# A Strassen-style down projection: when two residuals are formed, how block sums are spread over GpSimd's queue, and how the last norm is cut up

## The reference, cut to what matters

```python
def _rms(x, g):
    xf = x.astype(jnp.float32)
    y = xf * lax.rsqrt(jnp.mean(xf * xf, axis=-1, keepdims=True) + EPS)
    return (y * g.astype(jnp.float32)).astype(x.dtype)

def _layer(x, pos, l, ...):
    ...                                             # attention
    x = x + jnp.concatenate([y_diff, y_mla], axis=-1) @ w_o[l]
    h = _rms(x, ffn_norm[l])
    x = x + (jax.nn.silu(h @ w_gate[l]) * (h @ w_up[l])) @ w_down[l]
    return x
```

## Time and profile before

| | |
|---|---|
| median of 3 runs | 2282.66 us (2282.36 to 2284.16) |
| the profiled execution | 2283.84 us |
| its span | 2282.0 us |
| PE busy | 2238.9 us, 98% of the span |
| DVE busy | 1805.9 us, 79% |
| POOL busy | 993.2 us, 44% |
| ACT busy | 984.0 us, 43% |
| mean granted clock of TensorE | 0.993 of full speed |

### The profile page before, as it was taken

How to read it: one execution, slowest core, us unless ns; L and a number is a source line. 1 busy time by engine, 2 the same in 40 slices (tenths; PEclk the granted TensorE clock), 3 DMA queues, 4 the chain that set the end, 5 groups by cost and what they waited for, 6 DMA issues and landing times.

```text
span 2282.0 us, 31255 instructions
## 1 busy us (share of the span) xinstructions
PE 2238.9 (98%) x10600; PEld 1862.5 (82%) x10600; DVE 1805.9 (79%) x2794; ACT 984.0 (43%) x1876; POOL 993.2 (44%) x689
## 2 busy tenths in 40 slices
PE   8999999999999999999999999999999999999997
PEld 6888888888888888788888888888888888887886
DVE  6998388888787877989958873987966666679997
ACT  4556134544444444443324541455444444443442
POOL 4314100125777777788600010001255455577883
PEclk9999999999999999999999999999999999999998
DMA  8533542233666666843243136323323232376421
GB/s 305 219 110 135 198 168 91 93 130 127 223 221 234 221 234 232 330 138 103 92 148 111 56 130 221 111 74 111 120 79 111 97 110 97 110 261 241 139 72 77
DMA packets 93463, 346.89 MB, mean 152 GB/s; under 512 B 9760, under 2 KB 9888, under 8 KB 74016
## 3 DMA queue, kind: packets, MB, share of 16 engines
q1 hardware_dynamic: 92624, 344.53, 43.1%
q10 hardware_dynamic: 720, 0.86, 0.1%
HBM read 237.35 MB, written 108.00 MB: 151 GB/s over the span
## 4 chain that ended last, share of the span: by engine, by line
PE 85%; DVE 6%; issue 2%; POOL 1%; ACT 1%; DMA 0%; DVEq 0%; SPq 0%; ACTq 0%; POOLq 0%
PE bank L520 27%; PE bank L522 27%; PE bank L521 27%; PE bank L1162 2%; PE bank L1000 1%; PE bank L1008 1%; DVE x L2212 1%; DVE aT_lo L2031 1%; PE bank L526 1%; PE bank L527 1%; DVE u L2178 1%; DVE qpe L1906 1%; DMA raw<-in_wffn 0%; POOL slot L913 0%; DVE y_out L2314 0%
## 5 line engine op out<-in xcount | busy, mean ns | idle before, releaser
L898 POOL TENSOR_TENSOR slot<-raw,slot 128x512 fp32r<-128x512 f32 x160 | 223.3, 1399 | 234.4 <-ACT slot L1610 234.4
L520 PE MATMUL bank<-h_hi,slot 128*128 128x512 f32 x640 | 249.0, 389 | 0.0
L521 PE MATMUL bank<-h_lo,slot 128*128 128x512 f32 x640 | 249.0, 389 | 0.0
L522 PE MATMUL bank<-h_hi,slot 128*128 128x512 f32 x640 | 249.0, 389 | 0.0
L875 POOL TENSOR_TENSOR acc<-sq,zero 128x512 f32<-128x512 f32 x6 | 6.7, 1116 | 546.1 <-ACT sq L1399 546.1
L520 PE MATMUL bank<-u,slot 128*128 128x512 f32 x560 | 220.2, 393 | 7.8 <-POOL slot L913 7.0
L521 PE MATMUL bank<-u,slot 128*128 128x512 f32 x560 | 219.7, 392 | 0.0
L522 PE MATMUL bank<-u,slot 128*128 128x512 f32 x560 | 219.6, 392 | 0.0
L520 PE MATMUL bank<-h_hi,w 128*128 128x512 f32 x512 | 203.4, 397 | 0.0
L898 POOL TENSOR_TENSOR slot<-s_stage,slot 128x512 fp32r<-128x512 f32 x120 | 175.9, 1466 | 60.2 <-ACT slot L1610 58.7
L2212 DVE TENSOR_TENSOR x<-x,bank 128x512 f32<-128x512 f32 x280 | 177.5, 678 | 28.3 <-PE bank L522 28.3
(11 more groups left out here) (255 smaller groups left out, 5931.5 us busy)
## 6 DMA issues: line engine op xcount, KB each, us to landing
w<-parked SPq DMA_DIRECT2D x81, 1024.0 KB, 4.8
raw<-in_wffn SPq DMA_DIRECT2D x112, 512.0 KB, 3.4
u_kept<-made SPq DMA_DIRECT2D x148, 256.0 KB, 2.9
uf<-u_kept SPq DMA_DIRECT2D x70, 512.0 KB, 5.6
parked<-w SPq DMA_DIRECT2D x27, 1024.0 KB, 6.3
parked<-p SPq DMA_DIRECT2D x27, 1024.0 KB, 4.9
raw<-in_watt SPq DMA_DIRECT2D x27, 512.0 KB, 5.0
praw<-in_watt SPq DMA_DIRECT2D x27, 512.0 KB, 5.8
```

The source lines that it names most:

```text
L520: nc.tensor.matmul(out_ap, lhs[0], rhs[0], start=first, stop=False, skip_group_check=joins)
L521: nc.tensor.matmul(out_ap, lhs[0], rhs[1], start=False, stop=False, skip_group_check=joins)
L522: return nc.tensor.matmul(out_ap, lhs[1], rhs[0], start=False, stop=last, skip_group_check=joins)
L898: nc.gpsimd.tensor_tensor(slot[i][:, 1, :], gate_source(i), slot[i][:, 0, :].bitcast(F32), ALU.subtract).then_inc(s_gate_lo.sem, 1)
```

## The change

It has four parts.

1. `residual_sums` runs ahead of G1's addition instead of ahead of G4's. Its two halves are interleaved tile by tile, it reads x12 from `x` itself, and it waits for three of the four loads of `x` at once. The tile `x12`, its load and its semaphore are gone. G4's activations for round 1 are loaded where x12 was, at the end of the gate and up projections, and SP's wait for `residual_sums` is gone with them.
2. In every round POOL takes the eight block sums in another order: only the two of G5 ahead of G5's low parts, the other six behind G2's.
3. After the last round `sums_undone` and the first four plain additions alternate.
4. In the last layer the squares of request 0 go to tiles of their own and are added up half by POOL, half by DVE; their sum over partitions is taken on PE behind 2 plain tiles of request 1 (before: behind 6), the spread stands ahead of the 6th tile (before: behind the last), and DVE's outputs of request 0 stand between its plain additions. For request 1, PE adds the tiles 4 to 7 of the squares up itself in PSUM, and two small DVE operations and two DVE additions are gone.

```diff
-SUMS_BEFORE = 6
+SUMS_BEFORE = 2
+SPREAD_BEFORE = 5
...
                 if c == FC - 1:
-                    sp.dma_start(x12[:], x_kept[:, 1, 0:MH, :]).then_inc(s_x12, 16)
+                    load_u(l, 1, G4)
                     load_u(l, 1, N3)
...
                 next_u(G2)
-                if d == 0:
-                    sp.wait_ge(s_res.sem, s_res.layer_at(l, 2 * MH - 1))
-                    load_u(l, 1, G4)
                 next_raw(G7, 0)
...
-            def down_sums(l, d):
-                for q in range(2):
-                    a11, a21, a22 = down_source(q, G1), down_source(q, G7), down_source(q, G4)
-                    pool.wait_ge(s_down_raw[q][0], raw_value(l, d, q))
+            def down_weights(l, d):
+                ...
+                down_lo(l, d, G1)
+                for q, (a11, a21, a22) in enumerate(sources):
                     pool.wait_ge(s_down_raw[q][1], raw_value(l, d, q))
                     nc.gpsimd.tensor_tensor(a_sum[q][:], a21, a22, ALU.add).then_inc(s_a_sum.sem, 1)
+                down_lo(l, d, G5)
+                down_lo(l, d, G2)
+                for q, (a11, a21, a22) in enumerate(sources):
                     nc.gpsimd.tensor_tensor(a21, a11, a21, ALU.subtract).then_inc(s_a_sum.sem, 1)
...
-            def final_sums(squares):
+            def first_sums():
+                pe.wait_ge(s_acc_first, POOL_SQUARES - 1)
+                pe.wait_ge(s_acc_second, KT - POOL_SQUARES - 1)
                 for m in range(NT):
-                    last = nc.tensor.matmul(bank[0][:, m:m + 1], squares[:, m * P:(m + 1) * P], ones[:, 0:1], start=True,
+                    nc.tensor.matmul(bank[0][:, m:m + 1], acc_first[:, m * P:(m + 1) * P], ones[:, 0:1], start=True, stop=False)
+                    last = nc.tensor.matmul(bank[0][:, m:m + 1], acc_second[:, m * P:(m + 1) * P], ones[:, 0:1], start=False,
                                             stop=True)
...
                 def residual_sums():
-                    dve.wait_ge(s_x_in[2], 16 * (l + 1))
-                    dve.wait_ge(s_x_in[3], 16 * (l + 1))
+                    for n in (0, 2, 3):
+                        dve.wait_ge(s_x_in[n], 16 * (l + 1))
                     for m in range(MH):
-                        x21, x22 = x[:, 0, MH + m, :], x[:, 1, MH + m, :]
+                        x12_, x21, x22 = x[:, 1, m, :], x[:, 0, MH + m, :], x[:, 1, MH + m, :]
                         nc.vector.tensor_tensor(x21, x22, x21, ALU.subtract).then_inc(s_res.sem, 1)
-                    dve.wait_ge(s_x12, 16 * (l + 1))
-                    for m in range(MH):
-                        x22 = x[:, 1, MH + m, :]
-                        nc.vector.tensor_tensor(x22, x22, x12[:, m, :], ALU.subtract).then_inc(s_res.sem, 1)
+                        dve.wait_ge(s_res.sem, s_res.layer_at(l, 2 * m))
+                        nc.vector.tensor_tensor(x22, x22, x12_, ALU.subtract).then_inc(s_res.sem, 1)
...
                     for group in range(WP):
-                        if d == 0 and group == G4:
+                        if d == 0 and group == G1:
                             residual_sums()
                         added(d, group)
...
                 for m in range(MH):
                     sums_undone(m)
+                    down_add(m)
...
-            for k in range(6):
-                down_add(KT + k)
+            second_add(5)
+            second_add(6)
+            down_add(KT)
+            second_add(7)
+            down_add(KT + 1)
             rsqrt_column(final, D, bank[0][:, 0:NT], (s_pe, 1), s_final, root=rstd)
-            down_add(KT + 6)
-            down_add(KT + 7)
+            for k in range(2, 5):
+                down_add(KT + k)
             dve.wait_ge(s_pe, 2)
             output(0, 0)
+            down_add(KT + 5)
             output(0, 1)
+            down_add(KT + 6)
             output(0, 2)
-            final_add(4)
-            final_add(5)
-            for m in range(3, KT):
+            down_add(KT + 7)
+            for m in range(3, 6):
                 output(0, m)
-            ...
+            rsqrt_column(final, D, bank[3][:, 0:NT], (s_pe, 3), s_final)
+            output(0, 6)
+            output(0, 7)
```

More of the change, by code:

```diff
@@ L486, in encoder_trunk @@
         s_final_acc = sem("final_squares_added")
+        s_sq_first = sem("first_request_squares")
+        s_acc_first = sem("first_request_low_squares_added")
+        s_acc_second = sem("first_request_high_squares_added")
         s_y = sem("outputs_made")
@@ L977, in _ @@
                     last.then_inc(s_a_lo.sem, 1)
-                add_squares("next", l)
+                if l < L - 1:
+                    add_squares("next", l)
+            pool.wait_ge(s_sq_first, 2)
+            nc.gpsimd.tensor_tensor(acc_first[:], sq_first[:, 0, :], sq_first[:, 1, :], ALU.add).then_inc(s_acc_first, 1)
+            for k in range(2, POOL_SQUARES):
+                pool.wait_ge(s_sq_first, k + 1)
+                pool.wait_ge(s_acc_first, k - 1)
+                nc.gpsimd.tensor_tensor(acc_first[:], acc_first[:], sq_first[:, k, :], ALU.add).then_inc(s_acc_first, 1)
             pool.wait_ge(s_act, 2)
@@ L1301, in down_end @@
                         if l == L - 1 and b == 1 and n == SUMS_BEFORE:
-                            f, sq0, add0, st0, t0, x0 = norm_counts("next", l)
-                            pe.wait_ge(s_add.sem, f(s_add, add0 + KT - 1))
-                            final_sums(acc)
+                            first_sums()
+                        if l == L - 1 and b == 1 and n == SPREAD_BEFORE:
+                            spread((s_final, ROOT_LINKS), s_pe, rstd, 2)
                         plain_down(l, b, n)
-                if l == L - 1:
-                    spread((s_final, ROOT_LINKS), s_pe, rstd, 2)
             for l in range(L):
@@ L1350, in _, with last_sums @@
                 down_end(l)
-            def last_sums(squares, at):
+            def last_sums(squares):
                 for m in range(NT):
-                    last = nc.tensor.matmul(bank[at][:, m:m + 1], squares[:, m * P:(m + 1) * P], ones[:, 0:1], start=True,
-                                            stop=True)
-                last.then_inc(s_pe, 1)
-            pe.wait_ge(s_act, 7)
-            last_sums(sq_out[:, 6, :], 0)
-            pe.wait_ge(s_final_acc, 5)
-            last_sums(acc_out, 5)
-            pe.wait_ge(s_act, 8)
-            last_sums(sq_out[:, 7, :], 3)
-            spread((s_final, 2 * ROOT_LINKS + 2), s_pe, yy, 1)
+                    last = nc.tensor.matmul(bank[3][:, m:m + 1], squares[:, m * P:(m + 1) * P], ones[:, 0:1], start=False,
+                                            stop=True, skip_group_check=True)
+                return last
+            nc.tensor.matmul(bank[3][:, 0:NT], ident[:], zero[:].to_broadcast([P, NT]), start=True, stop=True)
+            pe.wait_ge(s_final_acc, POOL_SQUARES - 1)
+            last_sums(acc_out)
+            for k in range(POOL_SQUARES, KT):
+                pe.wait_ge(s_act, k + 1)
+                last = last_sums(sq_out[:, k, :])
+            last.then_inc(s_pe, 1)
+            spread((s_final, 2 * ROOT_LINKS), s_pe, yy, 1)
         @block.scalar
@@ L1768, in _ @@
                     last.then_inc(s_a_hi.sem, 1)
-                for k in range(KT):
-                    norm_square("next", l, 0, k)
-                    if l < L - 1:
+                if l < L - 1:
+                    for k in range(KT):
+                        norm_square("next", l, 0, k)
                         x_hi("next", l, 0, k)
+            act.wait_ge(s_prod.sem, s_prod.layer_at(L - 1, NPROD * ND - 1))
+            for k in range(KT):
+                act.wait_ge(s_xf.sem, s_xf.layer_at(L - 1, k))
+                nc.scalar.activation(sq_first[:, k, :], x[:, 0, k, :], ACT.Square).then_inc(s_sq_first, 1)
             for k in range(KT):
                 act.wait_ge(s_xf.sem, s_xf.layer_at(L - 1, KT + k))
-                act.wait_ge(s_prod.sem, s_prod.layer_at(L - 1, NPROD * ND - 1))
                 nc.scalar.activation(sq_out[:, k, :], x[:, 1, k, :], ACT.Square).then_inc(s_act, 1)
@@ L2289, in _ @@
                     sums_undone(m)
+                    down_add(m)
                 dve.wait_ge(s_back.sem, s_back.layer_at(l, 2 * MH - 1))
-                for ev in range(KT):
+                for ev in range(MH, KT):
                     down_add(ev)
@@ L2305, in final, with second_add @@
                 dve.wait_ge(s_final, n[0])
-            def final_add(k):
-                dve.wait_ge(s_act, k + 1)
-                dve.wait_ge(s_final_acc, k - 1)
-                nc.vector.tensor_tensor(acc_out[:], acc_out[:], sq_out[:, k, :], ALU.add).then_inc(s_final_acc, 1)
+            def second_add(k):
+                dve.wait_ge(s_sq_first, k + 1)
+                if k == POOL_SQUARES + 1:
+                    nc.vector.tensor_tensor(acc_second[:], sq_first[:, k - 1, :], sq_first[:, k, :], ALU.add).then_inc(
+                        s_acc_second, 1)
```

(3 more changed lines are left out.)

29 lines of the change are left out of this document (11 added, 18 removed).

## The result

The changed kernel takes **2298.1 us** (median of 6 runs, 2297.13 to 2299.78) where the kernel before, run beside it on the same chip, takes 2284.1: a ratio of 1.0063, interval 1.0053 to 1.0073. It is slower by 14.0 us; the forecast was 8.4 us slower, and 2298.1 lies above both the prediction's own range (2287 to 2295) and its wide one (2281 to 2298). 1.4 us of the gap between 2291.0 and 2298.1 is the kernel before itself, whose median was 2282.66 when the forecast was made and 2284.1 beside the changed kernel. The profiled execution took 2297.13 us, its span 2295.0.

What follows compares the result with a forecast made beforehand. PE, busy 98% of the span, was taken as the bound; -13.7 + 25.8 - 3.7 = +8.4 us gave 2292.2 from the profiled 2283.84, or 2291.0 against the median. Own range 2287 to 2295; 8 in 10, 2281 to 2298.

Steps and rivals of the forecast that it cites:

- 10.4 us of standing still in each layer: Round 0: PE starts G2 at 942.6 instead of 932.14, waiting for DVE's G1 addition behind eight residual operations.
- 6.7 forecast: Of DVE's eight residual operations ahead of G1's addition, 6.7 would cost 1.70 us each beside busy POOL.
- The clock behind it: Slow matmuls on PE at a low clock behind the wait ahead of G2: 2.5 us a layer.
- The term +25.8: Part 1's added cost: 2 x 12.9 us, from 10.4 us of waiting ahead of G2 plus 2.5 of clock a layer.
- -13.7: Parts 1 and 2 remove round 1's wait for POOL, its slow matmuls and some lag: 7.3 + 6.4 us.
- each of the two edits alone nearly covers the wait: Dropping SP's wait, or making G5's low parts 5 to 6.8 us earlier, nearly covers round 1's 3.35 and 3.68 us.
- -3.7 for the end: Part 4, end of layer 1: request 1's outputs begin at 2270.3 instead of 2274.02; bounds -2 and -5.
- last addition 0.9 with its signal, square on ACT 0.7, PE's last sums 1.1: Steps in us after PE's last plain tile at 2264.1, followed by small operations of 1.75 and two outputs of 1.4.
- Other rounds 0: Part 2 in the other rounds: POOL just in time for G4, by 0.3 us; taken as 0, upper bound 12 us.
- part 3 hidden: Part 3 is hidden in layer 0 behind PE's 16 plain tiles; layer 1's earlier squares are counted with part 4.

Runs made afterwards that it cites:

- pool_held: Changed kernel with G4's low parts right behind G2's and POOL, in round 0, waiting for the residual sums before its block sums; 2291.5 us.
- part1_undone: Changed kernel with part 1 taken back, parts 2, 3 and 4 kept; 2279.3 us, ratio 0.9981 to the kernel before.
- Part 2 alone: Kernel before with only POOL's new order of block sums, run twice; 2276.8 us and, again, 2277.3 us.
- pool_six: Changed kernel with POOL adding six squares of request 1 instead of four, so PE makes three passes of last sums instead of five; 2294.1 us.
- raw_ahead: Kernel before with SP issuing round 1's raw weights ahead of its wait for the residual sums; 2290.2 us, ratio 1.0025.
- part1_alone: Kernel before with part 1 only; 2296.7 us, ratio 1.0055.
- part2_end: Kernel before with part 2, POOL adding six squares of request 1, and request 0's last two outputs behind the inverse square root; 2277.2 us.
- sums_later: Changed kernel with the first sums over partitions behind 3 plain tiles of request 1 instead of 2; 2296.6 us.
- best3: best2 with the four residual operations on x22 moved behind G4's addition; 2286.7 us, ratio 1.0010.
- best1: Changed kernel without part 1, round 1's raw weights ahead of SP's wait, first sums behind 3 tiles, POOL adding six squares; 2285.2 us.
- best2: part1_undone with G4's low parts right behind G2's, first sums behind 3 tiles and POOL adding six squares; 2279.9 us.
- end_eased: Changed kernel with first sums behind 3 plain tiles instead of 2 and POOL adding six squares instead of four; 2295.8 us.

## Why the prediction was wrong in size

- **Direction and main mechanism: right.** 10.4 us of standing still in each layer was forecast, 10.42 measured in both, with seven residual operations at 1.7 us (6.7 forecast). pool_held shows the cause, part1_undone that part 1 brings it.
- **The clock behind it:** 2.5 us a layer was forecast. The 24 matmuls behind the wait took 7.07 and 7.36 us instead of 5.44, so 1.6 and 1.9. The term +25.8 was 24.4.
- **-13.7: the sum nearly right, its reason wrong.** Without the wait and the slow matmuls behind it the rounds of the changed kernel are 190.6 us in both layers, so 13.3 of the 13.7 are gone. But "each of the two edits alone nearly covers the wait" is false. Part 2 alone gets 4.4 and 2.5 us of it, run again 4.1 and 3.4. SP's wait taken out of the way, with the residuals left in their place, costs 5.7 us. In the changed kernel it did no harm because the residuals no longer stood ahead of the `made` operations: DVE did these from 956.46 on at 0.7 us, before POOL woke at 961.47. That the sum came out is partly luck, since the prediction did not look at this.
- **-3.7 for the end: the step that failed.** Measured +2.1, a miss of 5.9. The prediction's chain "last addition 0.9 with its signal, square on ACT 0.7, PE's last sums 1.1" counts one pass of last sums behind the last plain tile. The code has five there, since PE takes its instructions in order and the tiles stand ahead of all of them: they end 6.07 us behind the last plain tile, not 2.7, and 1.3 of that is the low clock. With a faster rest, the outputs of request 1 begin 9.1 us behind that tile, not 6.2: 2.9 us. Ahead of it, the plain tiles took 27.5 us, not 25.2: a wait of 1.57 us instead of 0.8 (counted from where the sums could have started, so it is a little more than the 1.41 of the row), 1.3 us of low clock that the sum left out, and 0.2 in smaller terms: 2.3 us. The last 0.7 lies between the last output and the end of the span. pool_six confirms the count: with three passes the last sums end 3.1 us behind the last plain tile.
- **Together:** the rounds cost 11.0 us where 12.1 was forecast, the end 2.1 where -3.7 was. The rounds outweigh the end, so the direction held although the sign of the end's term was wrong.
- **Other rounds 0, part 3 hidden:** no wait from round 1 on is in the trace, so POOL was in time for G4. Part 3 was not run alone; by the ends of 42.1 and 43.1 us above it gives about 1.0 in the end, which is not shown by a run of its own.

## What to carry to other kernels

An engine's idle stretch can be what lets its neighbour run fast: before a wait is removed, look at what will then run beside what. Where two engines slow each other, as DVE and POOL do here, moving or waking the one is priced by what the other has in its queue at that time. And behind the last tile count every instruction in the queue, not only the one whose data comes last.

## What the runs showed of the hardware

- DVE and POOL, both with two SBUF inputs of 128x512, take turns: about 1.7 us a step for each, against 0.6 to 0.7 (DVE) and 1.25 to 1.3 (POOL) alone (changed, pool_held, raw_ahead, part1_alone). A DVE operation of only 128x4 can pay nearly a whole POOL operation as well: 1.15 to 1.21 us instead of 0.16, for four of nine while POOL adds squares (part2_end). Three of the four have two operands in SBUF; one is a TENSOR_SCALAR, which has one.
- What the clock takes behind a wait does not follow the wait's length. Counted as the time of the 24 matmuls behind it above 5.44 us: 10.42 us of waiting cost 1.6 and 1.9 in the changed kernel, but 2.6 and 2.4 in sums_later, whose code is the same there; 3.35 us cost 3.0 and 3.68 us cost 1.8 in the kernel before; 2.63 us cost 1.7 in layer 0 of best3 and 0.1 in layer 1. What decides it stays open, so a forecast can carry such a term only as a range.
- TensorE's clock also fell, from 2.4 to 1.2 GHz, without any wait, behind 16 matmuls of 128x1 that kept PE busy for 1.9 us (sums_later, 0.56 granted; best1, 0.65); in best2, best3 and end_eased the same 16 were followed by the full clock (1.00), and end_eased has the code of sums_later up to there. Before, with 8 of them, it stayed up (1.00). What decides it stays open too.
